# A hybrid decoder trunk in float32: where the scores stand in TensorE's queue in the even mixer's attention loop

## The reference

```python
q, c_kv, q_i, k_i, w_i, gate_b, x_b = _split(h @ w_in, EVEN_SPLITS)
c_kv = rmsnorm(c_kv, kv_norm)
k = (c_kv @ w_uk).reshape(Bb, S, A_HEADS, A_HEAD_DIM)
v = (c_kv @ w_uv).reshape(Bb, S, A_HEADS, A_HEAD_DIM)
a_out = dsa_attention(q, k, v, q_i, k_i, w_i)      # 8 heads of 64, the 128 best-scored keys of each token
xc = causal_dwconv(x_b, conv_w, conv_b)
b_out = rg_lru(xc, w_ra, b_ra, w_ri, b_ri, lam) * jax.nn.gelu(gate_b)
return jnp.concatenate([a_out, b_out], axis=-1) @ w_out
```

## Time and profile before

| | |
|---|---|
| median of 3 runs | 2197.95 us |
| lowest and highest | 2197.67 and 2198.14 us |
| span of the profiled execution | 2196.3 us |
| median of the runs less that span | 1.65 us |
| instructions | 36637 |
| TensorE busy in the span | 2181.2 us |

### The profile page before, as it was taken

How to read it: one execution, slowest core, us unless ns; L and a number is a source line. 1 busy time by engine, 2 the same in 40 slices (tenths; PEclk the granted TensorE clock), 3 DMA queues, 4 the chain that set the end, 5 groups by cost and what they waited for, 6 DMA issues and landing times.

```text
span 2196.3 us, 36637 instructions
## 1 busy us (share of the span) xinstructions
PE 2181.2 (99%) x13844; PEld 1944.0 (89%) x13844; DVE 1456.1 (66%) x2185; ACT 1127.0 (51%) x1881; POOL 110.4 (5%) x104
## 2 busy tenths in 40 slices
PE   9999999999999999999999999999999999999999
PEld 8999888775888899998899998887868889999987
DVE  8888636788666598874388885345266656888732
ACT  6555524476554565563365554245345546555531
POOL 0000000675000000000000000000000000000000
PEclk9999999999999999999999999999999999999999
DMA  4332332221452233332323323322214422333322
GB/s 164 105 105 95 115 106 63 77 77 49 144 165 79 74 115 105 105 105 96 115 87 105 105 95 115 115 81 87 96 36 138 155 79 77 103 105 105 110 99 78
DMA packets 61953, 221.44 MB, mean 101 GB/s; under 512 B 7953, under 2 KB 8081, under 8 KB 61858
## 3 DMA queue, kind: packets, MB, share of 16 engines
q1 hardware_dynamic: 57456, 208.69, 28.9%
q10 hardware_dynamic: 4402, 11.46, 1.5%
HBM read 218.03 MB, written 2.10 MB: 100 GB/s over the span
## 4 chain that ended last, share of the span: by engine, by line
PE 93%; DVE 4%; ACT 1%; POOL 1%; issue 1%; DMA 0%; DVEq 0%; POOLq 0%
PE ps L2099 12%; PE ps L2100 12%; PE ps L2101 12%; PE ps L2195 11%; PE ps L2197 11%; PE ps L2196 11%; PE ps L479 6%; PE ps L480 6%; PE ps L481 6%; PE ps L2035 1%; DVE e_sc L1768 1%; DVE e_max L1767 1%; DVE e_sc L1783 1%; PE ps L2583 0%; PE ps L2560 0%
## 5 line engine op out<-in xcount | busy, mean ns | idle before, releaser
L417 DVE TENSOR_TENSOR w_lo<-w_raw,w_hi 128x1024 fp32r<-128x1024 f32 x204 | 252.5, 1241 | 358.2 <-ACT w_hi L412 357.3
L412 ACT ACTIVATE w_hi<-w_raw 128x1024 fp32r<-128x1024 f32 x210 | 221.6, 1057 | 311.4 <-PE ps L2197 225.4
L2099 PE MATMUL ps<-t_hi,w_hi 128*128 128x256 f32 x1280 | 362.3, 283 | 0.0
L2100 PE MATMUL ps<-t_lo,w_hi 128*128 128x256 f32 x1280 | 362.2, 283 | 0.0
L2101 PE MATMUL ps<-t_hi,w_lo 128*128 128x256 f32 x1280 | 362.2, 283 | 0.0
L2099 PE MATMUL ps<-x_hi,w_hi 128*128 128x256 f32 x960 | 271.7, 283 | 0.0
L2100 PE MATMUL ps<-x_lo,w_hi 128*128 128x256 f32 x960 | 271.7, 283 | 0.0
L2101 PE MATMUL ps<-x_hi,w_lo 128*128 128x256 f32 x960 | 271.7, 283 | 0.0
L1490 DVE TENSOR_TENSOR w_lo<-f,w_hi 128x1024 fp32r<-128x1024 f32 x152 | 186.2, 1225 | 124.0 <-ACT w_hi L840 124.0
L479 PE MATMUL ps<-x_hi,w_hi 128*128 128x256 f32 (+1 forms) x736 | 250.8, 341 | 1.6 <-DVE x_lo L1367 0.9
L480 PE MATMUL ps<-x_lo,w_hi 128*128 128x256 f32 (+1 forms) x736 | 246.0, 334 | 0.0
(11 more groups left out here) (352 smaller groups left out, 4317.8 us busy)
## 6 DMA issues: line engine op xcount, KB each, us to landing
w_raw<-in_wstream SPq DMA_DIRECT2D x310, 512.0 KB, 3.3
w_raw_odd<-in_wstream SPq DMA_DIRECT2D x80, 512.0 KB, 3.3
tmp<-in_post_gains ACTq DMA_DIRECT2D x8, 512.0 KB, 5.1
gain_bc<-in_gains ACTq DMA_DIRECT2D x7, 512.0 KB, 3.8
h<-in_x SPq DMA_DIRECT2D x4, 512.0 KB, 5.7
c_mem<-in_mem ACTq DMA_DIRECT2D x2, 1024.0 KB, 5.8
out_dram<-h SPq DMA_DIRECT2D x3, 512.0 KB, 2.7
c_gain<-in_mem_gains ACTq DMA_DIRECT2D x2, 512.0 KB, 7.5
```

The source lines that it names most:

```text
L412: nc.scalar.activation(weights(v)[0], raw(v), ACT.Copy).then_inc(w_hi_ready, 1)
L417: nc.vector.tensor_tensor(wl, raw(v), wh.bitcast(f32), ALU.subtract).then_inc(w_ready, 1)
L2099: nc.tensor.matmul(dst, wh[:, at], xh[:, b, :], start=first, stop=False, skip_group_check=True)
L2100: nc.tensor.matmul(dst, wh[:, at], xl[:, b, :], start=False, stop=False, skip_group_check=True)
```

## The change

In TensorE's loop the two lines that issue the scores of pair m move from the front of the iteration to behind the gate's blocks and the output piece. All other statements stand as they were, as do the queues of all other engines.

```diff
--- before.py
+++ after.py
@@ -2495,12 +2495,12 @@
 
                 BETWEEN = {10: (0, 0), 11: (0, 1), 12: (1, 0), 13: (1, 1), 14: (2, 0), 15: (2, 1), 16: (3, 0)}
                 for m in range(N // 2 + 1):
-                    if m < N // 2:
-                        scores(m)
                     if m < len(BESIDE):
                         blocks("gate", sum(BESIDE[:m]), BESIDE[m])
                     if m in BETWEEN:
                         out_tile(*BETWEEN[m])
+                    if m < N // 2:
+                        scores(m)
                     if m == 1:
                         pe.wait_ge(v_ready, V0[i] + 1)
                     if m == AH + 3:
```

## The result

The changed kernel takes 2203.01 us (2202.86 to 2204.97, 8 runs) against 2197.9 us (2197.23 to 2198.28, 8 runs) for the kernel before: a ratio of 1.0026 [1.0016, 1.0036], 5.1 us slower. The forecast was 2.8 us slower. Its sign was right, its size was not. The time lies at the upper end of the range that the bounds of the terms gave (2199.0 to 2203.0), and past the line of 0.2% on the side that had been given 0.19.

A forecast was written before the change was run, and what follows sets the result against it. TensorE's queue counts, at 99% busy, with VectorE the bound from pair 7's reduction on. Delays summed to +3.15 us, less 0.3 gave +2.8: 2197.95 to 2200.8 us, bounds 2199.0 to 2203.0, 8 in 10 within 2197.5 to 2203.4.

The forecast's parts named there:

- G(m): TensorE's gate blocks or output piece in iteration m; after the change no longer cover for pair m's chain.
- T(5): Transposes of pair 5 on TensorE: forecast at 510.75, delay 3.4 us, of which 1.2 is new idle time.
- S(3): TensorE's scores of iteration 3, S(m) being those of iteration m: forecast to start at 496.2.
- T(3): Transposes of pair 3 on TensorE: forecast at 501.6 after 1.6 us idle, delay 2.2 us.
- Rival 1: Cover was ample and TensorE only gains: 2.0 us less, 2196.0 us; chance 0.13.
- rival 2: Nothing much changes, as VectorE's bound and idle time take up most delay: -0.5 to +1, 2198.2 us; chance 0.14.
- Front: Start of the attention loop, up to S(3): first mixing some 0.5 us later, at 496.9 rather than 496.35.
- T(0): Transposes of pair 0 on TensorE: forecast to wait about 0.2 us, behind VectorE's first search round and split.
- port relief: VectorE, pair 7's reduction to pair 10's reciprocal: running later, it meets less of GpSimd; 1.3 us back, bounds 0 and 3.0.
- the 0.3 that I took off the sum: Correction to the sum: the same laying out on the old order ended 0.3 us later than its trace.
- Rival 4: No relief from GpSimd on VectorE, and pair 3's split runs beside GpSimd: +4.9 us, 2202.9 us; chance 0.12.
- Rival 3: Clock falls between 500 and 506, slowing the five blocks before pair 5's scores: +4.2 us, 2202.2 us; chance 0.13.

The follow-up runs named there:

- the front half: The kernel before with the new order only in iterations 0 to 9, beside the gate's blocks: 2201.43 us, 1.0017.
- The two kernels that took the wait of T(0) away: New order in all iterations but 0: 2204.66 us. Changed kernel with VectorE's first weight split moved behind pair 0's reciprocal: 2205.0 us.
- both moves: Changed kernel with the last search rounds one place earlier and VectorE's second gate split in iteration 5 instead of 6: 2204.04 us, 1.0028.

## Why the prediction was right or wrong

**Right.** The mechanism: TensorE's queue loses G(m) as cover, the transposes of pairs 3 and 5 start after idle times of 1.98 and 1.33 (forecast: 1.6 and 1.2), the waits of scores for reductions are gone, the first piece of the third output unit waits for the lowering. Single steps held closely. From S(5) to T(5) the forecast was 5.0 and the trace has 5.02 (506.86 to 511.88). From S(3) to T(3) it was 5.4, and is 5.66. From the reciprocal at the end of pair 10 to that of 541.62 before, 12.55 was carried over, and 12.55 it is (532.74 to 545.29); the prediction calls that row the reciprocal of pair 14, and it is the one that VectorE does in iteration 14, of pair 13, which changes no number. Rival 1 (the cover is ample) and rival 2 (VectorE takes the delay up) are out: the first by the four waits, the second by 3.6 us from the front half alone.

**The step that failed: *Front*.** It said that T(0) waits about 0.2. It waited 1.25. VectorE's first split ran at 486.60 beside a step of GpSimd and took 2.04. At the 1.21 of a lone split the wait would have been 0.4; the step priced no contention, and the bounds of the sum have none for this split. That, and an S(0) that came 0.2 late, put S(3) at 496.98, or 497.44 with the 0.46 of the entry, against the 496.2 of the forecast: 1.2 late. By the last mixing it is 2.3 late, so that this step holds about half of the miss. In times of the kernel before:

| | forecast | after (+0.46) | late by |
|---|---|---|---|
| S(3) | 496.2 | 497.44 | 1.2 |
| T(3) | 501.6 | 503.10 | 1.5 |
| S(5) | 505.75 | 507.32 | 1.6 |
| T(5) | 510.75 | 512.34 | 1.6 |
| reduction of pair 7 | 513.5 | 515.24 | 1.7 |
| reciprocal of pair 10 | 531.2 | 533.20 | 2.0 |
| last mixing, by the sum of 3.15 | 556.57 | 558.85 | 2.3 |

Three smaller misses follow. T(3) comes 5.66 after S(3) where I had 5.4, since the mask, also beside GpSimd, took 0.80 where I had 0.46. From the reduction of pair 7 to the reciprocal of pair 10 VectorE needed 17.96 (514.78 to 532.74), against 19.0 before, so 1.04 came back where 1.3 was forecast. That was not for want of *port relief*. Against lone durations its instructions there are stretched by 4.6 before and by 2.9 after, so 1.7 came back; but at 527.84 VectorE sat idle 0.55 for the scores of pair 10, which now stand behind an output piece that waits itself. The forecast had no such wait. With the scores of pairs 10 on in front, as in the kernel of the front half, the stretch took 17.70, the 1.3 of the forecast. The last 0.3 is the pieces' waits and constants: behind the reciprocal of pair 10 the forecast added 1.0, and it was 1.3. No row stands behind the 0.3 that I took off the sum for my laying out of the old order; without it the forecast would have been 3.15 against the 5.1 of the runs.

The prediction also says that VectorE has "hardly a wait" in those 19.0. It waits 1.72 of them for high parts of ScalarE, in both kernels alike, so that the difference stands, but its queue alone does not set that stretch.

**But the front term is not a sum's term.** The two kernels that took the wait of T(0) away brought the scores of pair 3 forward by 0.7 to 1.2 us, and their reciprocal of pair 3 came 21.5 and 22.4 us after the copy of the values, against 21.7 in the changed kernel. An earlier start met another step of GpSimd, and most or all of it was lost. So my forecast of T(3) probably held a second error that the first one hid. I had put S(3) 15.56 after the copy of the values (496.2 less 480.64), and in the kernel with the first scores in front it stands at 15.58: there the split was not the lone one of 1.21 that I chose, but took 2.16, and TensorE idled 2.96 and met the half clock. So the mis-sized wait names where the forecast parted from the profile, and not 1.05 us that could be had back. The general error lies behind the forecasts of both T(0) and T(3): VectorE's instructions were priced at their lone durations. Rival 4 (no port relief, and the split beside GpSimd, 2202.9) has the right time by luck: the split that met GpSimd was that of iteration 0, the one of pair 3 that it priced was alone (1.22), and the relief did come back. Rival 3 (the clock falls in the new place) did not happen in the changed kernel's profile, where the clock is 1.00 throughout; it did in the two kernels with the longer idle time in front of T(3).

The stretched rows: the same split takes 1.22 or up to 2.18, and the mask, a step in place on float32, 0.43, 0.80, 0.83, 1.47 or 1.50, by what GpSimd has under way when it starts. GpSimd's timeline of the changed kernel, beside the split of 486.60 and the mask of 499.92:

```profile
486.26 1.29 POOL L629 TENSOR_TENSOR tmp<-tmp,e_t 128x512 f32<-128x512 f32 x1
487.64 1.47 POOL L631 TENSOR_SCALAR f<-tmp 128x512 f32<-128x512 f32 x1
...
499.14 1.29 POOL L641 TENSOR_TENSOR e_t<-e_t,e_gate 128x512 f32<-128x512 f32 x1
```

The split starts with 0.95 of GpSimd's step still to run and loses 0.83; the mask starts with 0.51 to run and loses 0.37. GpSimd's next step, of 487.64, starts with 1.00 of the split to run and takes 1.47, where a like one takes 0.62. The split of the earlier trace rows (1.11 to run, 0.97 lost) and the masks and splits of pair 3 in the kernels with the first scores in front, with the first split moved and with the other layout of the gate's blocks behave alike: the loss is what is left of the other's step, less 0.12 to 0.15. The Trainium skill (SBUF — State Buffer, the section on the two sides of SBUF) says that VectorE, in a two-port mode or with two inputs in SBUF, and GpSimd take the shared port pair by an exclusive lock for a whole instruction; these rows agree. The cost is decided anew for each instruction, which fits that moving the chain by a microsecond moved its length by as much.

**What stays open.** Two of the 8 runs of the changed kernel are at 2204.9, and three of the 8 with the other layout of the gate's blocks at 2206; their mean clocks are listed lower (0.998 against 0.999 to 1.0 in the latter), which fits a fall of the clock in some executions only, but none of these was profiled. That 3.6 of the loss comes from the new order beside the gate's blocks is shown by the kernel that has it there alone. That it comes by lost cover rests on where the waits stand: each kernel that gave back cover or shortened a chain got little or nothing of the time back, so what a single wait costs stays open. A kernel with GpSimd's steps moved away, so that only the contention changes, was not tried; that it is the cause of the longer splits rests on the times above.

## What to carry to other kernels

Before a producer (here the scores) is moved behind filler work on the bounding engine, count from rows what each chain needs behind it, and how much filler still stands there: here two chains of 5.0 to 5.7 us had 3.7 left. Where two engines share a port, don't price an instruction by its lone duration because it seems to fall in a gap: work out the chain with the lone and with the stretched duration, and keep both as bounds until an experiment has moved the chain. Changes of shape saved on a busy engine brought nothing that could be measured where another engine set the pace, so test them in such a place first.

## What was not expected of the hardware

Removing an idle time can cost more than the idle time: two kernels in which TensorE reached the scores of pair 3 0.7 to 1.2 us sooner ended 1.65 and 2.0 us later than the changed kernel, by their medians. The granted clock fell to 0.50 within idle times of 2.96 and 3.40 in front of T(3), and fell after one of 1.8 in front of T(5) in the changed kernel with both moves. It stayed at 1.00 after 1.98 in front of T(3) in the changed kernel, and, with the split in iteration 4, after 2.00 in front of T(5), to fall after 1.97 in front of T(7). The length of the one idle time does not say whether it falls, and the rows don't show what does.
